# The first expert's code entered when its width is known, with the tail's squares, a bank and three small loads moved

## What is computed

```python
h = rmsnorm(x, norm1_g)
q, k, v, u = split(h @ w_in)                  # 512 columns each
o = diff_attention(q, k, v, lam, subln_g)     # 4 heads, causal, two softmax maps each
z = multiscale_pool(u, w_pool, b_pool, ...)   # trailing means of 2, 4, 8, 16 tokens
x = x + concat(o, z) @ w_out
h = rmsnorm(x, norm2_g)
logits = h @ router_w + router_b              # 32 experts
gates = softmax(top 4 of logits)
for each token, for its 4 experts e:
    gate = min(h @ w_gate[e] + b_gate[e], 7);  up = clip(h @ w_up[e] + b_up[e], -7, 7)
    y = gate * sigmoid(1.702 * gate) * (up + 1)
    x += gates[e] * (y @ w_down[e] + b_down[e])
out = rmsnorm(x, final_g)
```

## Time and profile before

| | |
|---|---|
| runs | 2072.96 us median of three (2072.66 to 2073.78) |
| profiled execution | 2074.92 us, its span 2073.2 |
| TensorE busy (PE) | 2011.8 us, 97% of the span |
| its weight loads (PEld) | 1643.8 us, 79% |
| DVE, ACT, POOL busy | 655.5 (32%), 283.8 (14%), 232.9 (11%) |
| packets of instructions, queues q8 and q14 | 113 and 38, 1.85 and 0.31 MB |

### The profile page before, as it was taken

How to read it: one execution, slowest core, us unless ns; L and a number is a source line. 1 busy time by engine, 2 the same in 40 slices (tenths; PEclk the granted TensorE clock), 3 DMA queues, 4 the chain that set the end, 5 groups by cost and what they waited for, 6 DMA issues and landing times.

```text
span 2073.2 us, 32125 instructions
## 1 busy us (share of the span) xinstructions
PE 2011.8 (97%) x13457; PEld 1643.8 (79%) x13458; DVE 655.5 (32%) x1363; ACT 283.8 (14%) x457; POOL 232.9 (11%) x381
## 2 busy tenths in 40 slices
PE   8999988996999999999999999999999999999996
PEld 4444455554998898889788999988888888989996
DVE  3115676443223222222222332222222222222223
ACT  2001245111011001101001010111010100100103
POOL 0001333212000001000001010010000000000103
PEclk9999999997999999999999999999999999999998
DMA  4210022214878879998999988899899998887855
GB/s 173 81 41 1 1 92 84 100 61 152 305 248 305 307 272 322 321 329 296 321 322 318 309 294 272 286 319 335 312 304 322 319 319 310 279 299 260 287 189 199
DMA packets 231449, 500.89 MB, mean 242 GB/s; under 512 B 7766, under 2 KB 8303, under 8 KB 231298
## 3 DMA queue, kind: packets, MB, share of 16 engines
q1 hardware_dynamic: 218880, 454.46, 61.0%
q0 software_dynamic: 12368, 44.26, 8.6%
q10 hardware_dynamic: 50, 0.01, 0.0%
HBM read 463.63 MB, written 35.13 MB: 241 GB/s over the span
## 4 chain that ended last, share of the span: by engine, by line
PE 72%; DMA 1%; DVE 1%; issue 1%; SPq 0%; ACT 0%; POOL 0%; POOLq 0%; DVEq 0%; ACTq 0%
PE ps L1694 57%; PE ps L1721 12%; PE ps L1708 2%; PE ps L1714 1%; PE ps L1701 1%; DMA qk<-x_rows 1%; DMA out<-qk 0%; DVE x L1254 0%; DMA hT<-h_rows,hT 0%; DMA x_rows<-x,hT 0%; DVE qk L1363 0%; SPq L439 0%; DVE xn L1221 0%; ACT hT L821 0%; ACT x L857 0%
## 5 line engine op out<-in xcount | busy, mean ns | idle before, releaser
L1694 PE MATMUL ps<-hT,qk 128*128 128x128 f32 (+8 forms) x4096 | 501.7, 284 | 6.8 <-issue 6.8
L1694 PEld LDWEIGHTS ps<-hT,qk 128*128 128x128 f32 x4096 | 493.5, 192 | 16.6 <-issue 16.0
L1721 PE MATMUL ps<-w_ring,hT 128*128 128x512 f32 x576 | 251.8, 593 | 0.0
L1694 PE MATMUL ps<-hT,u_all 128*128 128x128 f32 (+8 forms) x2048 | 247.7, 282 | 0.0
L1694 PE MATMUL ps<-hT,v 128*128 128x128 f32 (+8 forms) x2048 | 247.7, 282 | 0.0
L1694 PEld LDWEIGHTS ps<-hT,v 128*128 128x128 f32 x2048 | 244.6, 191 | 0.0
L1694 PEld LDWEIGHTS ps<-hT,u_all 128*128 128x128 f32 x2048 | 244.6, 191 | 0.0
L1694 PE MATMUL ps<-hT,w_ring 128*128 128x132 f32 (+7 forms) x1792 | 233.8, 291 | 5.0 <-DVE x L1254 3.6
L1694 PEld LDWEIGHTS ps<-hT,w_ring 128*128 128x128 f32 x1792 | 229.3, 190 | 7.4 <-issue 7.0
L1721 PEld LDWEIGHTS ps<-w_ring,hT 128*128 128x128 f32 x576 | 107.5, 190 | 126.7 <-issue 126.3
L558 POOL DMA_INDIRECT hT<-h_rows,hT x46 | 45.3, 986 | 1148.9 <-issue 672.1
(11 more groups left out here) (250 smaller groups left out, 1470.6 us busy)
## 6 DMA issues: line engine op xcount, KB each, us to landing
w_ring<-in_w_down SPq DMA_DIRECT2D x64, 2048.0 KB, 7.9
qk<-in_w_gate SPq DMA_DIRECT2D x32, 2048.0 KB
qk<-in_w_up SPq DMA_DIRECT2D x32, 2048.0 KB
v<-in_w_gate SPq DMA_DIRECT2D x32, 2048.0 KB, 10.5
u_all<-in_w_up SPq DMA_DIRECT2D x32, 2048.0 KB, 8.7
x<-in_b_down SPq DMA_DIRECT2D x32, 512.0 KB, 11.6
w_ring<-in_w_in SPq DMA_DIRECT2D x3, 2048.0 KB, 9.0
x<-in_x SPq DMA_DIRECT2D x8, 512.0 KB, 12.4
```

The costliest lines, as they stand in the source:

```text
L1694: ins = pe.matmul(bank[:, m, 0:n], w[g][:, k, m * P:(m + 1) * P], rhs[:, k, 0:n], start=k == 0, stop=k == KC - 1)
L1721: ins = pe.matmul(ps[:, 2 * (g % PAIRS), :], aT[:, k, 0:P], w[g][:, k, :], start=k == 0, stop=k == KC - 1)
```

## The change

Six edits in one diff:

- TensorE enters the first expert's body as soon as its width is loaded. The hints and their tree are gone for this jump; the body itself begins with a block, under a branch that is taken around when the expert's number is not 0, which does the gate part of the index and turns the gathered rows (both halves, or for the narrow body the first alone). Every one of the eleven bodies holds this block. `turn_second` is gone.
- `squares_of_rows` on ACT does blocks 0 to 3, and DVE squares blocks 4 to 7 itself, in the last item ahead of the roots.
- In the last item `down(0)` stands behind the roots, and all rows that DVE norms, block 7 among them, come ahead of `down(1)`.
- v's and u's jobs take banks 3 and 1 in turn where they took 1 and 3.
- The three bias tables are loaded into three areas of their own and their DMAs are issued ahead of the sixth block's x1 store, without the wait for the output products.
- A junk area is moved to make room.

```diff
...
         x1T = xn[:, 1].rearrange("p (k t) -> p k t", t=P)
         h2 = [hT[:, 6], hT[:, 7], xn[:, 2], xn[:, 3]]
 
-        junk_h, ss_h = xn[:, 4], lam[:, 6:7]
+        junk_h, ss_h = xn[:, 0], lam[:, 6:7]
         late = xn[:, 6:8].rearrange("p a n -> p (a n)")
         r = Routes()
         r.slot = late[:, 0:256].rearrange("p (b e) -> p b e", e=E)
...
         xg = of_hT(2, D)
         xT, aT = of_hT(KC, SLOTS), of_hT(KC, SLOTS)
 
-        bias_rows = flat[0:E, 2 * D:2 * D + 3 * D].rearrange("p (i n) -> p i n", i=3)
+        bias_rows = [xn[0:E, 5], hT[0:E, 4], xn[0:E, 4]]
         gt, ut, sg = (of_hT(4, SLOTS) for _ in range(3))
         tok = of_hT(TB, 6, dt=BF16)
         tab = [of_hT(4, dt=I32) for _ in range(3)]
...
 
         x2 = qk[:, :, :, :].rearrange("p a (b c) n -> p (a b) (c n)", c=2)
 
-        junk_f, x_last = x[:, 7], xg
+        junk_f, junk_v, x_last = x[:, 7], xn[:, 3], xg
         small_f = x[:, 4, MORE * E:MORE * E + 10]
         ss_l, rstd_l, tmp_l = small_f[:, 0:2], small_f[:, 2:4], small_f[:, 4:10].rearrange("p (i h) -> p i h", h=2)
 
...
 
             if n == len(jobs) - 1:
                 return 6
-            return n % 8 if n < first_late else (1, 3)[(n - first_late) % 2]
+            return n % 8 if n < first_late else (3, 1)[(n - first_late) % 2]
 
         def user_before(n):
 
...
                 sp.wait_ge(o_done, TB)
                 sp.dma_start(w[2], weights(0, 2)).then_inc(w_ready[2], 16)
                 for b in range(TB):
-                    if b == TB - 1:
-                        sp.wait_ge(out_mm, 2 * TB)
+                    if b == TB // 2 + 1:
                         for i, bias in enumerate((d["b_gate"], d["b_up"], d["b_down"])):
-                            sp.dma_start(bias_rows[:, i, :], bias[0]).then_inc(biases_in, 16)
+                            sp.dma_start(bias_rows[i], bias[0]).then_inc(biases_in, 16)
                     sp.wait_ge(x1_ready, 2 * (b + 1))
                     sp.dma_start(rows.x1[b * P:(b + 1) * P, :], x[:, b, :]).then_inc(x1_st[b], 16)
                     sp.wait_ge(h2_ready, b + 1)
...
                         turn_in(j + 1)
 
                 def squares_of_rows(again):
-                    for b in range(TB):
+
+                    for b in range(TB if again else TB // 2):
                         act.wait_ge(x_in[b], 32 + 16 * again)
                         if b or again:
-                            act.wait_ge(squares_f, again * TB + b)
+                            act.wait_ge(squares_f, again * (TB // 2) + b)
                         act.activation(junk_f, x2[:, b, :], ACT.Square, accum_out=ss[:, b:b + 1]).then_inc(squares_f, 1)
 
                 squares_of_rows(0)
...
                 for b in range(SCALED):
                     act.wait_ge(times_g, b + 1)
                     act.activation(x2[:, b, :], x2[:, b, :], ACT.Copy, scale=rstd[:, b:b + 1]).then_inc(ready_a, 1)
-                act.wait_ge(squares_f, TB)
+                act.wait_ge(squares_f, TB // 2)
                 act.sem_inc(passed, 1)
 
                 def squares_of_last(nh):
...
 
                 def last_rows(nh):
 
-                    normed_row(TB - 1)
                     dve.wait_ge(last_in, 32)
                     last_tab = tab[(E - 1) % 3]
                     for h in range(nh):
...
                     for c in range(2):
                         gate_in(E - 1, n, c)
                         up_in(E - 1, n, c)
-                    down(0)
                     f.n = 0
                     f.did(dve.memset(ss_l, 1.0))
+                    for b in range(TB // 2, TB):
+                        dve.wait_ge(x_in[b], 32)
+                        f.need()
+                        f.did(dve.tensor_tensor_reduce(junk_v, x2[:, b, :], x2[:, b, :], 1.0, 0.0, ALU.mult, ALU.add,
+                                                       accum_out=ss[:, b:b + 1]))
                     dve.wait_ge(gf_in, 16)
-                    dve.wait_ge(squares_f, TB)
+                    dve.wait_ge(squares_f, TB // 2)
                     rsqrt_mean_dve(dve, f, rstd[:, :], ss[:, :], tmp[:, :, :], D)
                     f.need()
                     dve.sem_inc(rstd_f, 1)
-                    for b in range(SCALED, TB - 1):
+                    down(0)
+                    for b in range(SCALED, TB):
                         normed_row(b)
                     down(1)
                     last_rows(nh)
                 past_first(dve, wide, item)
 
                 def all_rows():
-                    dve.wait_ge(squares_f, 2 * TB)
+                    dve.wait_ge(squares_f, TB // 2 + TB)
                     g = Order(dve, order_f, f.n + STEPS_L)
                     rsqrt_mean_dve(dve, g, rstd[:, :], ss[:, :], tmp[:, :, :], D)
                     g.need()
...
                 def turn_bias(i, at):
                     pe.wait_ge(biases_in, 48)
                     for m in range(KC):
-                        ins = pe.transpose(ps[:, at, m * E:(m + 1) * E], bias_rows[:, i, m * P:(m + 1) * P], ident[0:E, 0:E])
+                        ins = pe.transpose(ps[:, at, m * E:(m + 1) * E], bias_rows[i][:, m * P:(m + 1) * P], ident[0:E, 0:E])
                     ins.then_inc(bias_mm, 1)
 
                 turn_bias(0, 4)
...
                     for k in ks:
                         ins = pe.matmul(ps[:, 2 * (g % PAIRS), :], aT[:, k, 0:P], w[g][:, k, :], start=k == 0, stop=k == KC - 1)
                     return ins
-
-                def turn_second(e, wide):
-                    with pe.If(wide > 0):
-                        pe.wait_ge(xT_ready, 2 * e + 1)
-                        pe.sem_inc(passed, 1)
-                        turn_in(1).then_inc(turn_mm[1], 1)
-                    with pe.Else():
-                        pe.sem_inc(turn_mm[1], 1)
 
                 def first_index(cols):
 
...
                         pe.wait_ge(pair_free, e * GROUPS + g + 1)
                         pe.sem_inc(passed, 1)
 
+                    with pe.If(e < 1):
+                        pe.wait_ge(gates_done, TB)
+                        pe.wait_ge(idx_ready, 1)
+                        first_index(slice(2, 6)).then_inc(gate_mm, 1)
+                        pe.wait_ge(gate_read, 1)
+                        pe.wait_ge(first_in, 16)
+                        turn_in(0).then_inc(turn_mm[0], 1)
+                        pe.wait_ge(gathered, 32)
+                        pe.sem_inc(passed, 1)
+                        if i:
+                            pe.wait_ge(xT_ready, 1)
+                            turn_in(1).then_inc(turn_mm[1], 1)
+                        else:
+                            pe.sem_inc(turn_mm[1], 1)
                     pe.wait_ge(xT_ready, e * 2 + 2)
                     ready(0)
                     product(0, xT).then_inc(group_done, 1)
...
                 start = nc.switch_bb("experts_start")
                 pe.wait_ge(widths_ready, 1)
                 pe.sem_inc(passed, 1)
-                first, first_hints = width_of(pe, 0), {}
-                call(first_hints, first, 0, len(WIDTHS) - 1)
-                pe.wait_ge(gates_done, TB)
-                pe.wait_ge(idx_ready, 1)
-                first_index(slice(2, 6)).then_inc(gate_mm, 1)
-                pe.wait_ge(gate_read, 1)
-                pe.wait_ge(first_in, 16)
-                turn_in(0).then_inc(turn_mm[0], 1)
-                pe.wait_ge(gathered, 32)
-                pe.sem_inc(passed, 1)
-                turn_second(0, first)
-                choose("first", first, first_hints, len(WIDTHS) - 1)
+
+                choose("first", width_of(pe, 0), {}, len(WIDTHS) - 1)
                 for i, n in enumerate(WIDTHS):
                     with nc.body(place[i], parent=start, valid_engines=[pe.engine]):
                         expert(i, n)
```

## The result

The changed kernel took 2096.37 us (median of 4 runs, 2092.68 to 2100.86), the kernel before 2073.37 on the same chip: ratio 1.0113, interval 1.0101 to 1.0125. The direction was the forecast's; 2096.4 lies far outside its range of 2068 to 2085. The forecast had +4.7 us, the measurement says +23.0. Its profiled execution was the slowest of the four, 2100.86 us, with a span of 2099.1 against 2073.2: +25.9.

What follows compares the result with a forecast made beforehand. TensorE was taken to bound the kernel, holding 72% of the chain of waits. Terms of -4.0, -0.9, 0, +1.0, +0.6 and +8.0 us summed to +4.7, giving 2077.7 us for the median, range 2068.0 to 2085.0.

Steps and rivals of the forecast that it cites:

- Term 1: First expert on TensorE: entering its code early starts its products sooner, -4.0 us, between 1.1 and 8 gained.
- Term 2: v's first block: no more wait for DVE to empty its bank, -0.9 us, bounds 0 and -0.9.
- Term 3: Bias loads: the 0.39 us wait saved goes into the rank product's wait; zero, within 0.4 us.
- Term 4: Tail: halving the squares saves nothing and costs 0.2, down(0) delays the first row; +1.0 us, bounds -0.2 and +2.3.
- Term 5: Experts 1 to 31: jumping over the first expert's block costs 0.3 us at two entries, +0.6 us.
- Term 6: Narrow bodies behind wider experts: a code page ends near the skip's end, stalling TensorE at six entries, +8.0 us.
- my upper price: Page's end in narrow bodies: first product at entry + 3.6 us if the page waits like a late jump.
- the lower price: Page's end in narrow bodies: first product at entry + 2.2 us, since a page already on its way made no wait.
- the two sums: Loss over the six narrow entries behind wider experts: 7.4 us by the lower price, 15.8 by the upper.
- Rival C: Code pages: one on its way is treated as asked for by a jump, 15.8 us lost, 2085.5 us; chance 0.11.
- Rival A: Code pages: no stall at the page's end, the skip lands in a page already there, 2069.7 us; chance 0.33.

Runs made afterwards that it cites:

- run 6: Kernel before with the change's v banks and bias loads, first expert's block in eleven copies behind all bodies, entered early: 2071.45 us, ratio 0.9984.
- run 9: Changed kernel with the old tail, first expert's block ahead of each body, filler keeping bodies' old places within 256: 2069.75 us, ratio 0.9984.
- run 8: Kernel before with only the order of down(0) and the rows in the tail changed: 2074.21 us, ratio 1.0005.
- run 7: Changed kernel without the first expert's part, POOL's four tail products made to wait for the roots: 2079.64 us, ratio 1.0032.
- run 3: Changed kernel with 129 never-executed instructions put ahead of the eleven bodies: 2092.74 us.
- run 4: Changed kernel with each width's first-expert block directly ahead of its body, so no branch and no skip: 2099.76 us.
- run 10: Kernel of run 9 with 64 more never-executed instructions ahead of all bodies: 2081.36 us, ratio 1.0039.
- run 11: Kernel of run 9 with all places 192 further, which is 64 less within 256: 2075.04 us, ratio 1.0011.
- run 1: Kernel before with the first expert's part of the change alone: 2091.9 us, ratio 1.0078.
- run 5: Kernel before with 129 never-executed instructions put ahead of its bodies, one more compare executed: 2077.71 us, ratio 1.0019.
- run 2: Changed kernel with the first expert's part undone, the other five edits kept: 2078.26 us, ratio 1.0021.

## Why the prediction failed

**Term 1, the first expert: right, and too small.** -4.0 was forecast. 6.1 came in the trace, and the width was loaded only 0.45 earlier than before, so -5.6 belongs here. The term that was mis-sized is the cold jump: I gave it 6.12 by the earlier trace rows, it took 3.58, and in runs 6 and 9 the same kind of jump took 3.90 and 3.35. Why it is shorter there than at 507 us stays open. The 6.1 of the old jump was met again in run 6 (6.21), for its second jump. The clock came back with the earlier start: granted 0.62 in 507 to 514 and 1.00 in 514 to 521, where the earlier trace rows has 0.50 until 520.

**Term 2, v's bank: -0.9 forecast, right.** v's products ran with no wait in the changed kernel, and the stretch from TensorE's product 300 to 440 took 51.6 us in place of 52.7: -1.1. 0.6 of it was lost again by the load of the width, in that one execution. The nine profiles with both the new bank and the new bias loads have that load at 494.2 to 495.7, the four without at 495.0 to 496.7.

```profile
126.34 4.03 PE L1465 MATMUL ps<-w_ring,hT 128*128 128x512 f32 x9
```

**Term 3, the biases: zero, right as far as the rows go.** The 0.39 went into the rank product's wait, 1.35 where the earlier trace rows has 0.90. No run has them alone.

```profile
493.02 0.21 PE L1634 MATMUL ps<-member,tri 128*128 128x32 bf16 x1 [1.35 <-DVE member L1118]
```

**Term 4, the tail: wrong.** The failed step is "DVE has the same last two: 1.226 us each". That row is from 5.9 to 20 us, where POOL did nothing of the kind. Here POOL was at its four products, and the square took 8.51. I never laid POOL's products beside DVE's squares. What was forecast for the order, +1.0, stood (run 8, and the 1.0 behind the roots in the trace); the squares cost 4.9 where I had 0.2. Run 7 shows the cause and its two-sidedness: whichever engine is moved, the other pays. In the kernel before DVE had only `down(0)` in that stretch, which reads PSUM and took its usual 0.96.

The Trainium skill has the rule (SBUF — State Buffer, Who interferes with whom): a DVE instruction with two inputs in SBUF contends with a GpSimd instruction that reads SBUF, by an exclusive lock, and the order of issue decides who blocks. The trace agrees, with one addition: each product took 2.35 us, but the square, whose record begins during the first, ended only behind all four, while in run 7 the two engines took turns. I had not looked for it; this rule spoke against the change.

**Term 5, the skip: right in size.** The branch itself took 0.22 to 0.25 us at the late entries, where I had 0.3. From entry to first product 0.8 us in place of 0.4 (947.4 to 948.19 against 948.9 to 949.35), so 0.4 at each late entry; but six entries were late, not two. It is part of the late entries' sum above.

**Term 6, the pages: wrong.** It is the step that I called the one that decides, and it did; its working failed in three ways. The place was nearly right: I had the skip's end within 10 instructions of a page's end, it is 27 ahead of it (3751 and 3778).

First, the price of that page. I took its packet's start as in the kernel before, 0.7 us after entry, at all six narrow entries behind wider experts. At 9 and 21 it started 3.7 us after. At the other four (2, 5, 17 and 27) it started 0.6 to 1.1 us after, as forecast, and there the product behind the page's end stood at entry + 3.2 to + 3.5, near my upper price of 3.6 and not the 2.2 that I took. It cost 0.44 us at expert 17 and under 0.1 at the others, because the eleven products ahead of the page's end and the lead covered it. At every such stop over 0.2 us, in the changed kernel and in runs 3, 4, 10 and 11, the next product began 2.4 to 2.8 us after its page's packet, much as a jump goes on 2.5 us behind its own: my reason for the lower price, that a page on its way and entered in sequence makes no wait, was wrong. (By the leads as I gave them the two sums are 7.1 and 15.5, not 7.4 and 15.8.) Why the packet was late at 9 and 21 is open. Behind wider experts the packets' starts among the queue's records go together with it in these two kernels: where the jump began before its target's packet (by 0.03 to 1.8 us, at experts 1, 9, 15 and 21) the next page's packet began 3.2 to 3.8 us after entry; where it began behind it (16 and 31, and 9 and 21 in the kernel before), 0.6 to 0.7. It is no rule: wider experts behind narrow ones (4, 8, 20 and 26, in both kernels) have the next packet 3.3 to 3.8 us after entry although the jump began behind its target's packet, and expert 15 in run 1 and expert 2 in run 5 go against it too. So 7.8 us of stops came from two experts and not 8.0 from six; the sums agree by luck.

Second, and this is the largest: "counted on, no wider body's skip comes near an end" looked at the skip alone. Every hint, every sequence behind it and every jump of the moved bodies lies elsewhere in its page too, and whether a jump finds its target's code depends on that. The late entries are 10.4 us that no term had. Run 5, the old bodies moved by 129 and 4.4 us slower, and runs 9 to 11, one program at three places and 11.6 us apart, show it with next to nothing else changed (one compare in run 5). In run 3 the skip itself waited for code, in wider bodies.

Third, TensorE came back from the stops at half rate: 7.7 us. I had weighed the clock at the start only.

Rival C had the price of the page right, a product about 2.5 us behind its packet, but neither the 27 instructions ahead of the page's end, which hid most of it at four entries, nor the late packet at the other two; it, too, had the clock and the late entries at nothing. Rival A, no stall at a page's end, is what run 9 made true by moving the code; that it measured the 2069.7 forecast for A is chance, since it has the old tail.

**What stays open.** When exactly the sequencer asks for a page, and which hints it heeds. The hint to the first expert was not heeded in the kernel before (placed at 498.0, no packet until 511.0), nor in run 6; between a hint and its target's packet lay 3.2 to 4.1 us for wider experts behind narrow ones and mostly 6.6 to 8.9 behind wider ones. I can say from the traces which entries were late, not compute it for a new layout.

## What to carry to other kernels

Where a program branches at run time, count the code like data: an edit that lengthens or moves a body moves every page's end in all that follow, and its cost can't be read from the instructions added. Try the same program at a few places before the edit is judged, or give bodies a fixed place within 256 instructions; here that turned the early entry from +18.5 us (run 1) into part of a gain of 3.2 (run 9). And before work goes over to DVE or POOL, lay it beside what the other one does in SBUF at that time.

## What the runs showed of the hardware that was not expected

- A page of TensorE's code ends every 256 instructions, to the instruction: stops ahead of 3778 in three programs (the changed kernel, runs 1 and 4), of 7874, 4034 and 8642 in three others (runs 3, 11 and 10), labels not counted.
- The jump into code that is not there took 3.35 to 3.90 us at 496 us (eight programs) and 5.40 to 6.21 at 505 to 508 (six programs).
- Behind a page's end the next product began 2.4 to 2.8 us after the page's packet, whether the packet began 0.6 or 4.1 us after entry.
- The taken branch over the first expert's block took 0.21 to 0.37 us in the changed kernel, and up to 5.9 us in run 3, where every body lies half a page further on.
- DVE's square waited through four POOL products (8.51 us, 8.78 in run 2), though the last three of them began while the square was waiting; in run 7 the two alternated at 3.3 us each.
- Stops of TensorE of 1.75 and 3.84 us within 7 us brought the granted clock to 0.50 for more than 4 us of back-to-back products.
